# One-hot products of the experts' weights in one pass of TensorE, prepared two groups ahead, with GpSimd making part of the weights' low parts

## What is computed

```python
q = (hb @ w_q).reshape(PEER_BLOCK, PEER_HEADS, 2, PEER_HALF)       # 8 heads, 2 halves
sc = jnp.einsum('thcd,hcnd->thcn', q, sub_keys)                     # 128 keys per half
s1, i1 = lax.top_k(sc[:, :, 0], 16)
s2, i2 = lax.top_k(sc[:, :, 1], 16)
cand_s = (s1[..., :, None] + s2[..., None, :]).reshape(..., 256)
top_s, pos = lax.top_k(cand_s, 16)                                  # 16 experts per head
idx = take(i1 * 128 + i2, pos)
g = softmax(top_s)
act = gelu(einsum('thkd,td->thk', u_tab[idx], hb))
out = einsum('thk,thkd->td', g * act, v_tab[idx])
```

## Time and profile before

| | |
|---|---|
| median of 3 runs | 3405.82 us (3403.29 to 3408.12) |
| the profiled execution | 3407.45 us, of which the profile's span is 3405.7 us |
| TensorE (PE) busy | 3253.8 us, 96% |
| weight loads (PEld) | 2663.0 us, 78% |
| DVE busy | 1926.9 us, 57% |
| ACT busy | 1232.9 us, 36% |
| POOL busy | 439.6 us, 13% |
| share of PE in the chain that ended last | 86% |

### The profile page before, as it was taken

The page is one execution under the profiler, slowest core; times in us unless marked ns, Lnnn a source line. Parts: engine busy times, 40 slices in busy tenths (PEclk is TensorE's granted clock), DMA queues, the critical chain, the costliest instruction groups (busy, mean ns, idle before and its releaser), DMA issues.

```text
span 3405.7 us, 37836 instructions
## 1 busy us (share of the span) xinstructions
PE 3253.8 (96%) x14880; PEld 2663.0 (78%) x14880; DVE 1926.9 (57%) x3440; ACT 1232.9 (36%) x1770; POOL 439.6 (13%) x516
## 2 busy tenths in 40 slices
PE   7989999999999999999999999999999977899999
PEld 6767777778888878888788888887888855688887
DVE  5654444567777776665555555555444567544443
ACT  4663444432222235555322222223222233532221
POOL 0000000020000007885000000002000344030000
PEclk9999999899999999999999999999999986799999
DMA  4323111324443445778855555542333310022331
GB/s 139 92 87 100 56 56 56 126 93 129 143 137 126 129 135 158 191 197 204 295 194 195 194 198 198 198 148 75 99 99 99 115 62 13 13 74 99 99 99 62
DMA packets 271199, 424.21 MB, mean 125 GB/s; under 512 B 144816, under 2 KB 148400, under 8 KB 271024
## 3 DMA queue, kind: packets, MB, share of 16 engines
q1 hardware_dynamic: 271024, 421.80, 39.1%
HBM read 348.87 MB, written 72.88 MB: 124 GB/s over the span
## 4 chain that ended last, share of the span: by engine, by line
PE 86%; DVE 7%; ACT 5%; POOL 1%; issue 1%; DMA 1%; SPq 0%; POOLq 0%; ACTq 0%
PE pb L539 27%; PE pb L540 27%; PE pb L541 27%; PE pb L819 3%; ACT scr L1051 2%; DVE S L1486 1%; DVE ST L1494 1%; ACT S L1054 1%; DVE ST L1486 1%; DVE whl L1486 1%; ACT L1051 1%; POOL pad L2018 0%; POOL pad L2015 0%; ACT whl L1054 0%; DVE scr L1494 0%
## 5 line engine op out<-in xcount | busy, mean ns | idle before, releaser
L539 PE MATMUL pb<-H,whl 128*128 128x512 f32 x2416 | 992.2, 411 | 24.2 <-DVE whl L1486 11.6
L540 PE MATMUL pb<-H,whl 128*128 128x512 f32 x2416 | 953.7, 395 | 0.0
L541 PE MATMUL pb<-H,whl 128*128 128x512 f32 x2416 | 953.1, 394 | 0.0
L1486 DVE TENSOR_TENSOR whl<-raw,whl 128x1024 fp32r<-128x1024 f32 (+4 forms) x550 | 649.6, 1195 | 436.8 <-ACT whl L1054 434.7
L1054 ACT ACTIVATE whl<-raw 128x1024 fp32r<-128x1024 f32 (+4 forms) x550 | 543.9, 1003 | 466.2 <-PE pb L541 465.9
L539 PE MATMUL pb<-S,whl 128*128 128x512 f32 (+1 forms) x1716 | 670.2, 391 | 18.8 <-DVE whl L1486 11.7
L540 PE MATMUL pb<-S,whl 128*128 128x512 f32 (+1 forms) x1716 | 667.9, 389 | 0.0
L541 PE MATMUL pb<-S,whl 128*128 128x512 f32 (+1 forms) x1716 | 667.6, 389 | 0.0
L539 PEld LDWEIGHTS pb<-H,whl 128*128 128x128 f32 x2416 | 462.1, 191 | 117.5 <-DVE whl L1486 13.7
L541 PEld LDWEIGHTS pb<-H,whl 128*128 128x128 f32 x2416 | 460.8, 191 | 99.1
L540 PEld LDWEIGHTS pb<-H,whl 128*128 128x128 f32 x2416 | 462.5, 191 | 85.4 <-issue 3.4
(11 more groups left out here) (186 smaller groups left out, 2739.5 us busy)
## 6 DMA issues: line engine op xcount, KB each, us to landing
raw<-in_pu SPq DMA_DIRECT2D x128, 512.0 KB, 3.9
raw<-in_pv SPq DMA_DIRECT2D x128, 512.0 KB, 4.5
raw<-in_w_in SPq DMA_DIRECT2D x72, 512.0 KB, 3.7
ad<-scr SPq DMA_DIRECT2D x128, 256.0 KB, 4.2
gd<-ST SPq DMA_DIRECT2D x8, 4096.0 KB, 21.3
GA<-gd SPq DMA_DIRECT2D x60, 512.0 KB, 4.6
GA<-ad SPq DMA_DIRECT2D x60, 512.0 KB, 6.3
raw<-in_wg SPq DMA_DIRECT2D x44, 512.0 KB, 3.3
```

Source lines behind the costliest of these rows:

```text
L539: e.matmul(o, lh, h, start=start, stop=False, skip_group_check=True)
L540: e.matmul(o, lh, l, start=False, stop=False, skip_group_check=True)
L541: return e.matmul(o, ll, h, start=False, stop=stop, skip_group_check=True)
L1486: return e.tensor_tensor(o, x, y, op)
```

## The change

1. Each group has four matmuls of float32r with 256 moving columns instead of four float32 matmuls of 128. The stationary operand is the plain one-hot `hot2`; the moving one holds, beside each other, `hot1` times the high part of the share and `hot1` times its low part (`share`). A group's result is 1024 columns in two banks; DVE adds the two halves and writes `stage` in one TENSOR_REDUCE (step `put` goes from ACT to DVE).
2. DVE makes `hot2` of a group in one instruction of 512 columns, and the `share` of the fourth token in two of 128. POOL makes `hot1` of three tokens in every group, and ACT scales these into `share` with six activations of 128 columns. There are two buffers, so this is made two groups ahead. ACT makes the high parts of all shares (`share_hi`), DVE the low parts.
3. POOL makes the low parts of all 16 `w_pq` units, of `pu` units below 48, and of every fourth one from there to 119 (`pool_makes_low`). Waits for low parts go through `low(j)`. POOL's `experts()` starts behind `squares("2")`.
4. `peer_order`: for heads 1 to 7 there are 10, 3, 7 and 5 u steps around `pq` and `sk` instead of 16, 8, 16 and 8; 6 instead of 8 behind `cand`, `best` and each `pick`; 34 instead of 20 behind `soft`. So 472 instead of 280 u steps stand between the products, and 11 instead of 9 units come after them. `soft` comes at u step 415 instead of 640.
5. In `ffn("3")` the sum over squares stands behind the gate product of i = 1, no longer inside `two()`.

```diff
+def pool_makes_low(unit):
+    name, i, _ = unit
+    return name == "w_pq" or name == "pu" and (i < 48 or i < 120 and i % 4 == 0)
...
-            u(16)
+            u(16 if h == 0 else 7 if c else 10)
             out.append(("sk", h, c))
-            u(8)
+            u(8 if h == 0 else 5 if c else 3)
         for step in (("cand", h), ("best", h), ("pick", h, 0), ("pick", h, 1)):
             out.append(step)
-            u(8)
+            u(6)
     out.append(("soft",))
-    u(20)
+    u(34)
...
-    left = 8 * (128 - s // 8 - 9)
+    left = 8 * (128 - s // 8 - 11)
...
     for q in range(128):
-        if q + 3 < 128:
-            out.append(("rows", q + 3))
-        for k in range(4 * q, 4 * q + 4):
-            out.append(("g", k))
-            if k % 4 == 3 and q:
-                out.append(("put", q - 1))
-            u((k + 1) * left // 512 - k * left // 512)
+        out.append(("g", q))
+        if q < 126:
+            out.append(("rows", q + 2))
+        out.append(("put", q))
+        u((q + 1) * left // 128 - q * left // 128)
...
+        def low(j):
+            return pool_lo if pool_makes_low(units[j]) else w_lo, ("low", j)
...
 tensor:
-                        if n % 4 < 3:
-                            q.wait_ge(pool, ("hot1", k))
-                        q.wait_ge(dve, ("hot2", k))
-                        last = e.matmul(b[:, c], hot2[n % 4][:, c], hot1[n % 4][:, c], start=True, stop=True, skip_group_check=True)
+                        q.wait_ge(dve, ("put", n - 3) if n > 2 else ("top", 15))
+                        q.wait_ge(dve, ("hot2", n))
+                        q.wait_ge(act, ("share", n))
+                        for u in range(4):
+                            last = e.matmul(bank[b + u // 2][:, 256 * (u % 2):256 * (u % 2) + 256],
+                                            hot2[n % 2][:, 128 * u:128 * u + 128], share[n % 2][:, 256 * u:256 * u + 256],
+                                            start=True, stop=True, skip_group_check=True)
...
-                            two(j, (bank[0], bank[2]), Hh, Hl, hx, (("gate", tag, 0), ("up", tag, 0)), tag)
+                            two(j, (bank[0], bank[2]), Hh, Hl, hx, (("gate", tag, 0), ("up", tag, 0)), tag if tag == "5" else None)
                             continue
                         linear(j, bank[i % 2], Hh, Hl, hx, ("gate", tag, i))
+                        if i == 1 and tag == "3":
+                            sum_of(tag)
...
 scalar:
+                    elif what == "rows":
+                        n = step[1]
+                        if n > 1:
+                            q.wait_ge(prod, ("g", n - 2))
+                        else:
+                            q.wait_ge(dve, ("over", 2))
+                        q.wait_ge(pool, ("hot1", n))
+                        q.wait_ge(act, "share_hi")
+                        for u in range(3):
+                            for part in range(2):
+                                s = (high_share, low_share)[part](4 * n + u)
+                                last = e.activation(hot_share(n, u, part), hot1[n % 2][:, 128 * u:128 * u + 128], ACT.Copy, scale=s)
...
 vector:
+                        tt(hot2[n % 2].rearrange("p (u i) -> p u i", u=4), iota.unsqueeze(1).to_broadcast([128, 4, 128]),
+                           I2[:, 4 * n:4 * n + 4].unsqueeze(2).to_broadcast([128, 4, 128]), ALU.is_equal)
+                        k = 4 * n + 3
+                        ts(hot_share(n, 3, 0), iota, I1[:, k:k + 1], ALU.is_equal, high_share(k), ALU.mult)
+                        ts(hot_share(n, 3, 1), iota, I1[:, k:k + 1], ALU.is_equal, low_share(k), ALU.mult).then_inc(
+                            dve.up(("hot2", n)), 1)
+                    elif what == "put":
...
+                        b = 512 * gbank[n % 3]
+                        e.tensor_reduce(stage[n // 16 % 2][:, :, 4 * g:4 * g + 4].rearrange("p i u -> p u i"),
+                                        pb_t[:, b:b + 1024].rearrange("p (u e i) -> p u i e", u=4, e=2), AX_X, ALU.add
+                                        ).then_inc(dve.up(("put", n)), 1)
...
 gpsimd:
+            def split(upto):
+                while lo_done[0] < min(upto, len(units)):
+                    j = lo_done[0]
+                    lo_done[0] += 1
+                    if pool_makes_low(units[j]):
+                        q.wait_ge(w_hi, j + 1)
+                        e.tensor_tensor(wlo(j), raw(j), f(whi(j)), ALU.subtract).then_inc(pool_lo.up(("low", j)), 1)
+
+            def experts():
+                for step in choice:
+                    what = step[0]
+                    if what == "pq":
+                        split(unit_at["w_pq", 2 * step[1] + step[2]] + NW - 1)
+                    elif what == "u" and step[1] % 8 == 0:
+                        split(unit_at["pu", step[1] // 8] + NW - 1)
+                    elif what == "rows":
+                        n = step[1]
+                        q.wait_ge(dve, ("over", 1))
+                        if n > 1:
+                            q.wait_ge(act, ("share", n - 2))
+                        for u in range(3):
+                            last = e.tensor_scalar(hot1[n % 2][:, 128 * u:128 * u + 128], iota,
+                                                   I1[:, 4 * n + u:4 * n + u + 1], None, ALU.is_equal)
+                        last.then_inc(pool.up(("hot1", n)), 1)
...
             squares("2", X, lambda k: (dve, ("x", "1", k)))
+            experts()
```

More of the change, by code:

```diff
@@ L383, in build @@
         ST_t, _ = at("ST", 16384, F32, offset=s_off)
-        scr_t, _ = at("scr", 10 * 512, F32)
-        pad_t, _ = at("pad", 2 * 544, F32)
+        scr_t, scr_off = at("scr", 10 * 512, F32)
+        share_t, _ = at("share", 2048, F32R, offset=scr_off + 4 * 1536)
+        high_t, _ = at("high", 512, F32R, offset=scr_off + 4 * 1024)
+        pad_t, pad_off = at("pad", 2 * 544, F32)
+        hot_t, _ = at("hot", 2 * 544, F32R, offset=pad_off)
         cst_t, _ = at("cst", NC_, F32)
@@ L394, in build @@
         assert pos[0] <= nc.sbuf_usable_end
-        pb = [ctx.enter_context(nc.psum_tensor(f"pb{i}", [128, 512], F32)) for i in range(8)]
-        bank = [pb[i][:, :] for i in range(8)]
+        pb_t = ctx.enter_context(nc.psum_tensor("pb", [128, 4096], F32))
+        bank = [pb_t[:, 512 * i:512 * i + 512] for i in range(8)]
         gd = nc.dram_tensor("gd", [128, 128, 512], F32).ap()
@@ L475, in build, with hot_share, high_share, low_share @@
         I1v, I2v, TSv = (z.rearrange("p (b h k) -> p b h k", b=4, h=8) for z in (I1, I2, TS))
-        hot1 = scr[3:7]
-        hot2 = [pad[0][:, 0:512], pad[1][:, 0:512], cos_t[:, 0:512], cos_t[:, 512:1024]]
+        hot1 = [cos_t[:, 384 * i:384 * i + 384] for i in range(2)]
+        hot2 = [hot_t[:, 544 * i:544 * i + 512] for i in range(2)]
+        share = cut(share_t, 2, 1024)
+        lows = [cos_t[:, 768:1024], sm_t[:, 0:256]]
         stage = [ST[:, 8192 * i:8192 * i + 8192].rearrange("p (i t) -> p i t", i=128) for i in range(2)]
-        gbank = [4, 5, 2, 3]
+        gbank = [4, 6, 2]
+        def hot_share(n, u, part):
+            return share[n % 2][:, 256 * u + 128 * part:256 * u + 128 * part + 128]
+        def high_share(k):
+            return f(high_t[:, k:k + 1])
+        def low_share(k):
+            return lows[k // 256][:, k % 256:k % 256 + 1]
         def ga(p):
@@ L808, in experts @@
                     elif what == "g":
[L809 to L814, removed]
-                            q.wait_ge(dve, ("top", 15))
-                        if n % 4 < 3:
-                            q.wait_ge(pool, ("hot1", k))
-                        q.wait_ge(dve, ("hot2", k))
-                        last = e.matmul(b[:, c], hot2[n % 4][:, c], hot1[n % 4][:, c], start=True, stop=True, skip_group_check=True)
-                        if k % 4 == 3:
-                            last.then_inc(prod.up(("g", n)), 1)
+                        n = step[1]
+                        b = gbank[n % 3]
+                        q.wait_ge(dve, ("put", n - 3) if n > 2 else ("top", 15))
[5 more added lines that the diff above has]
+                                            start=True, stop=True, skip_group_check=True)
+                        last.then_inc(prod.up(("g", n)), 1)
                 for g in range(16):
@@ L1289, in experts @@
                         run(ACT.Exp, TS, TS).then_inc(act.up("shares"), 1)
-                    elif what == "put":
+                    elif step == ("over", 2):
+                        q.wait_ge(prod, ("over", 2))
+                        copy(high_t[:, :], bank[6]).then_inc(act.up("share_hi"), 1)
+                    elif what == "rows":
                         n = step[1]
-                        g = n % 16
-                        q.wait_ge(prod, ("g", n))
-                        if g == 0 and n > 31:
-                            q.wait_ge(g_out[n // 16 % 2], ("g", n // 16 - 2))
```

(15 more changed lines are left out.)

53 lines of the change are left out of this document (21 added, 32 removed).

## The result

The changed kernel takes **3425.45 us** in the median (3423.52 to 3426.54) against 3405.82 before: the ratio is 1.0056, with an interval of 1.0042 to 1.0071. Forecast was 3365. The changed kernel is slower by 19.6 us, and the forecast was wrong by 60 us and in its sign. One execution of experiment 10 (13518 us) and one of the kernel before (8272 us) were in a disturbed state and are left out.

A forecast was written before the change was run, and what follows sets the result against it. PE, busy 96% of the span, was taken to bound the kernel. Terms -56 + 4 + 9.8 + 3 + 6.5 - 8 = -40.7 from the 3405.8 median gave 3365 us, range 3346 to 3415.

The forecast's parts named there:

- the products themselves: One-hot products: 512 float32r matmuls at 0.12 us instead of 0.23 save 56 us if PE sets the pace.
- waits among the products: One-hot products: +4 us for groups that wait all the same and for the change between kinds of matmul.
- start: Where the experts begin: POOL's low part comes late behind its squares, so the sum follows later, +9.8 us (+7 to +14).
- choice, `soft`, first product: From the heads' choice to the first product: +3 us at heads 1 to 7 and +6.5 at `soft`.
- behind the products: After the last product: no term of its own, counted as 0.
- `ffn("3")`: The sum's wait of 6.2 us for POOL's squares goes, with about 2 us of lower clock: -8 us.
- The step that failed: Products: two buffers give a group of slack for a group with a low part; +4 us for remaining waits and matmul changes.
- Nothing for the rest.: SP's stores and loads, waits for low parts, shares at `over`: no cost, as DMA is less pressed and lookahead covers delays.
- The choice: Heads 1 to 7: POOL's low parts slow DVE, 0.5 us late at each of six heads, +3 us (0 to +22).
- `soft`: At `soft`: PE waits 11.1 us for ACT instead of 4.6, +6.5 us (+4 to +9).
- rivals 1 and 2: Products' reduce: 1, reads pay, 2.24 us, total 3462, 15%; 2, writes pay, 1.73 us, total 3397, 10%.
- Rival 3: Choice: contention, low parts at 4.2 us, +22 for +3 at six heads, +14 at the start, total 3388; 13%.

The follow-up runs named there:

- experiment 10: The kernel of experiment 7 with all low parts made by DVE: 3376.77 us, 0.9913 of the kernel before.
- experiment 12: Changed kernel with POOL's low parts among the products and SP's loads two units later, and 4 MB stores in four pieces: 3391.14 us, 0.9952.
- experiment 7: Changed kernel: no POOL low parts among products, first two units' on DVE, u steps moved from behind `soft`, 4 MB stores in four pieces; 3353.10 us, 0.9848.
- Experiment 11: Changed kernel with only the 4 MB stores cut in four pieces: 3414.60 us, 1.0026 of the kernel before.
- experiment 3: Changed kernel with the low parts of the first two `w_pq` and `pu` units made by DVE again: 3411.66 us, 1.0012 of the kernel before.
- experiment 4: Changed kernel with 20 of the 34 u steps behind `soft` moved ahead of it: 3410.98 us, 1.0012 of the kernel before.
- Experiment 8: Kernel before, with only the sum of `ffn("3")` moved behind the gate product of i = 1: 3397.98 us, 0.9978.

## Why the prediction was wrong

The bill, in places of the two profiled executions:

| term | forecast | measured | how |
|---|---|---|---|
| the products themselves | -56 | -52.1 | without waits (experiment 12) 383.7 - 468 steps of 0.68; before, 307.3 - 279 such steps |
| waits among the products | +4 | +38.0 | stage 421.7 against 383.7 |
| start | +9.8 | +12.0 | sum at 726.84 against 714.84 |
| choice, `soft`, first product | +9.5 | +30.1 | sum to first product 464.5, against 577.9 less 211 steps of 0.68 |
| behind the products | 0 | +0.6 | last product to the first of `pv` 65.4 with 89 steps, 49.8 with 67 before, less 22 steps of 0.68 |
| `ffn("3")` | -8 | -9.7 | from there to the end 1746.3 against 1756.0 |
| sum | -40.7 | +18.9 | spans: +19.0 |

(Of the 472 steps 4 stand behind the last product, of the 280 before 1.)

- **The step that failed** is the sentence "The two buffers give a group of slack for a group with a low part in it", and its +4. It compared sums over a group (DVE 2.73, POOL 2.3, ACT 2.54 against 2.99) and took slack for granted. That PE can set the pace was right: experiments 7 and 12 reach 383.8 and 383.7 us, where the prediction's prices give 379.6 for the 468 steps and 511 products in between. The 4 us over that are a product at 0.128 instead of 0.12, about what the +4 had in it for the change between kinds of matmul; for waits it left nothing. POOL's sum of 2.3 was low (its 0.86 of a group of 3.0 is 2.6), but still under PE's. What failed is the slack: POOL came to a low part earlier than ACT to its high part, stood there 3.2 to 6.8 us, and so used up in waiting the lead that the buffers could have given. Experiment 12 gets all of the stage's 38 us back without taking work away; of them 27.3 were PE's idle time as the profile counts it, some 7 low clock (0.98, 1.00, 0.98 and 0.97 in the four windows of 100 us), and the rest lies around the stops.
- **"Nothing for the rest."** failed too. "SP: the 4 MB stores leave every 48 us instead of 38, so DMA is less pressed than at 0.70" looked at bytes, and DMA was not less pressed either: 0.8 in experiments 7 and 12. The queue's order counts: the issue behind a 4 MB store, mostly an `ad` store, took 14.4 to 19.0 us. It took 13.4 to 17.5 in the kernel before too, where PE waited for nothing among the products; so what is new is that such a delay reaches PE. That it does because less slack is left at ACT and POOL is argued, not measured. Experiment 11 puts the stores' part at 12 of the 38 us.
- **The choice** was right in mechanism and too small in size. Forecast was half a microsecond at each of six heads; measured 11.6 us in seven waits. I took POOL's hold on DVE as 2.1 us a head, evenly spread; it comes as 2.0 or 4.2 at single places, and a head with two in a row (4.4) isn't paid back by heads without. Behind the waits of 2.2 and 4.4 the granted clock was 0.94 over 60 us each, 7 us together, which I had not counted. With `soft`'s +7.7 and a wait of 2.1 at the first product, which the prediction doesn't have, this makes 28.4 of the 30.1.
- **Start, `soft` and `ffn("3")`** were right. At the start forecast +9.8, measured +12.0 between the two profiled executions (10.9 between the means of seven with and seven without); experiment 3 got 13.8 back by undoing only this. At `soft` the forecast was a wait of 11.1, measured 12.08; experiment 4 removed it. Experiment 8 gives `ffn("3")` alone -7.8.
- **The rivals.** The reduce took 1.214 us (128 of them), so rivals 1 and 2 are out. The Trainium skill, Vector Engine (DVE) Microarchitecture Reference, section "5.2 Measured stream behaviour on trn2", makes an exception for one source that alternates between two regions with one write for two reads. The trace agrees with that exception, here with reads 512 bytes apart in PSUM, and not with the 1.8 estimated from the section's rule. Rival 3 had contention in the choice, from low parts at 4.2 us: its size (+22 at the heads) came nearer to the measured 19 than the forecast's +3 did, though a low part took 2.42. No rival had the waits among the products, so none had the case that came.

The change as such is good: its products save 52 us, and 3353 is reached without touching them.

## What to carry to other kernels

When work is given to an idle engine, that engine's share of busy time says nothing about the place: look at what the engine's in-order program will stand for there, and what urgent work is queued behind. In the products of this kernel, an engine had to reach an operation when its input had long been made, not as early as possible, and each queue that waits for the result (here SP's loads, with the stores behind them) had to be moved with it. A large store is worth cutting into pieces if small, urgent transfers follow it in the same queue (here 12 us of the stage in experiment 11, 9 in experiment 7).

## What was not expected of the hardware

- A float32 GpSimd instruction with two inputs held DVE's casts, multiplications and one-hots until it ended (0.23 became 2.22, 0.39 became 2.42), but not every instruction: the eleven reduces from PSUM that overlapped such an instruction took 1.21 to 1.22, as all 128 did (1.21 to 1.23).
- GpSimd's subtraction of 1024 columns took 2.42 us in the mean of 82; DVE's with the same operands took 1.23.
- The issue of a small DMA behind a store of 4 MB in pieces of 256 bytes took 14.4 to 19.0 us on SP, behind 1 MB of the same 2.5 to 6.4.
